# Key pages of the decode, loaded and scored by halves of their buffer during prompt attention

## The reference

```python
k_past = cache_k[page_table, layer].reshape(db, past, N_HEADS_A, HEAD_DIM)
...
s = jnp.einsum('bqhd,bkhd->bhqk', q, k, preferred_element_type=jnp.float32) * ATTN_SCALE
s = s + jnp.swapaxes(c_q, 1, 2)[:, :, :, None] - jnp.swapaxes(c_k, 1, 2)[:, :, None, :]
s = jnp.where(k_pos[None, :] <= q_pos[:, None], s, -jnp.inf)
p = jax.nn.softmax(s, axis=-1)
```

## Time and profile before

| | us |
|---|---|
| three runs | 1713.23, 1716.95, 1719.72 |
| median | 1716.95 |
| the profiled execution | 1712.27 |
| its span (first to last instruction) | 1710.4 |
| TensorE busy with matmuls | 1623.9 (95%) |
| TensorE loading weights | 977.1 |
| DVE, ACT, POOL busy | 805.5, 486.5, 121.1 |
| mean granted clock of TensorE | 0.984 of full |

### The profile page before, as it was taken

How to read it: one execution, slowest core, us unless ns; L and a number is a source line. 1 busy time by engine, 2 the same in 40 slices (tenths; PEclk the granted TensorE clock), 3 DMA queues, 4 the chain that set the end, 5 groups by cost and what they waited for, 6 DMA issues and landing times.

```text
span 1710.4 us, 32596 instructions
## 1 busy us (share of the span) xinstructions
PE 1623.9 (95%) x13510; PEld 977.1 (57%) x13510; DVE 805.5 (47%) x1778; ACT 486.5 (28%) x948; POOL 121.1 (7%) x166
## 2 busy tenths in 40 slices
PE   6999999999999999999989989989999998999998
PEld 3555555555555555568655655568788853444443
DVE  5560299963222244441166665534545556333332
ACT  5301100001024532400155654443233462010001
POOL 1100100011100000100000000000000002122220
PEclk9999999999999999999989999999999999999999
DMA  6233231247631305573075455577575478799983
GB/s 257 90 110 123 100 123 39 75 138 193 189 106 60 124 40 223 215 254 119 16 236 158 127 159 152 152 227 230 163 220 175 152 274 310 282 326 351 349 316 129
DMA packets 150893, 302.87 MB, mean 177 GB/s; under 512 B 16821, under 2 KB 121477, under 8 KB 132374
## 3 DMA queue, kind: packets, MB, share of 16 engines
q1 hardware_dynamic: 128810, 155.65, 29.1%
q0 software_dynamic: 17280, 117.18, 19.2%
q10 hardware_dynamic: 4656, 27.96, 4.0%
HBM read 237.88 MB, written 65.10 MB: 177 GB/s over the span
## 4 chain that ended last, share of the span: by engine, by line
PE 67%; DVE 14%; DMA 6%; SPq 5%; ACT 4%; issue 3%; ACTq 0%; DVEq 0%
PE psum L854 29%; PE psum L1106 21%; DVE big L1871 9%; SPq L578 4%; PE psum L1069 4%; PE psum L935 4%; PE psum L825 3%; PE psum L1030 2%; PE psum L1055 2%; PE psum L880 2%; DMA big<-in_k_pages 1%; ACT big L1530 1%; DMA zst<-in_x_prompt 1%; DMA big<-in_aux 1%; PE psum L1314 1%
## 5 line engine op out<-in xcount | busy, mean ns | idle before, releaser
L854 PE MATMUL psum<-big,wbuf 128*128 128x416 f32 x1920 | 677.4, 514 | 12.2 <-DVE big L1777 11.0
L854 PEld LDWEIGHTS psum<-big,wbuf 128*128 128x128 f32 x1920 | 365.4, 191 | 318.7 <-issue 313.9
L1106 PE MATMUL psum<-big 64*64 64x64 f32 (+3 forms) x5456 | 266.0, 273 | 19.8 <-DVE big L2307 6.5
L1106 PEld LDWEIGHTS psum<-big 64*64 64x64 f32 (+2 forms) x5456 | 183.4, 134 | 108.5 <-issue 75.1
L1503 ACT ACTIVATE zst<-psum 128x416 f32<-128x416 f32 x123 | 63.0, 517 | 533.5 <-PE psum L854 533.4
L1871 DVE SCALAR_TENSOR_TENSOR big<-big,pars 128x2048 f32<-128x2048 f32 x120 | 148.2, 1298 | 1.1
L725 POOL DMA_INDIRECT big<-in_cache_v,pidx x64 | 63.8, 997 | 718.4 <-PE psum L1069 485.6
L825 PE MATMUL psum<-ident,big 128*128 128x128 f32 (+1 forms) x556 | 79.7, 283 | 12.1 <-ACT big L1734 4.0
L1760 ACT ACTIVATE big<-zst 128x1024 f32<-128x1024 f32 (+1 forms) x17 | 17.3, 1020 | 257.4 <-DVE zst L2395 207.7
L2395 DVE TENSOR_TENSOR zst<-zst,psum 128x512 f32<-128x512 f32 x49 | 33.7, 688 | 106.3 <-PE psum L1106 80.0
L825 PEld LDWEIGHTS psum<-ident,big 128*128 128x128 f32 (+1 forms) x556 | 61.8, 146 | 29.4 <-issue 12.7
(11 more groups left out here) (306 smaller groups left out, 1697.3 us busy)
## 6 DMA issues: line engine op xcount, KB each, us to landing
big<-in_k_pages SPq DMA_DIRECT2D x432, 128.0 KB, 2.3
zT<-zst ACTq DMA_DIRECT2D x25, 1040.0 KB, 6.1
wbuf<-in_w_slots SPq DMA_DIRECT2D x24, 512.0 KB, 4.1
big<-zT POOLq DMA_DIRECT2D x11, 1024.0 KB, 5.4
zst<-in_k_pages SPq DMA_DIRECT2D x80, 128.0 KB, 2.7
rwS<-big POOLq DMA_DIRECT2D x8, 1024.0 KB, 4.2
big<-rwS SPq DMA_DIRECT2D x8, 1024.0 KB, 5.7
zst<-in_x_prompt SPq DMA_DIRECT2D x16, 512.0 KB
```

Of the source, the lines that this page charges most:

```text
L854: last = nc.tensor.matmul(psum[:, m % CHUNKS, 0:CW], w[:, k, :], x, start=(k == 0), stop=(k == KT - 1))
L1106: return nc.tensor.matmul(out, l, r, start=start, stop=stop, skip_group_check=True)
```

## The change

Each early key step is cut in two. The first half takes the eight matmuls of the even sequences, the second those of the odd ones.

- SP: the 16 page numbers of a step are read into registers before any wait. Then SP waits until the first eight matmuls of the step in the buffer are done (`k_half`) and issues the eight pages of the even sequences; then it waits for `sc_mm` as before and issues the eight odd ones. The two halves are counted on semaphores of their own. Both are semaphores used earlier in the program (`x_in[4]`, `lf_stored`; `k_half` is `ss_mm`), so before the first early load SP now also waits for an old transfer of `lf_stored`.
- TensorE: the first half stands one block earlier in the item, behind the transposes of the last but one block and what follows them. It carries the waits for `o_read` and for DVE's reading of the step before. The second half stands where the whole step stood, and waits for its own eight pages alone.
- The order of the 16 matmuls, the 16 pages and their sizes, and the other 16 key steps are unchanged.

```diff
+        k_early_in, K_EARLY0 = (x_in[4], lf_stored), (X_SEEN[4], 16 * DEC_BATCH + 16)
+        k_half, K_HALF0 = ss_mm, CHUNKS
...
             def key_pages(k):
-                if k < KEARLY:
-                    if k > 0:
-                        sp.wait_ge(sc_mm, k)
-                elif k - KEARLY >= NRING:
+                if k - KEARLY >= NRING:
                     sp.wait_ge(sc_mm, k - NRING + 1)
...
+                if k < KEARLY:
+                    for half in range(2):
+                        if k > 0:
+                            sp.wait_ge(*((k_half, K_HALF0 + k) if half == 0 else (sc_mm, k)))
+                        for n in range(half, 16, 2):
+                            page_load(k_early, n, k_early_in[half])
...
-            def key_step(k, bank, pages):
-                if k > 0:
+            def key_step(k, bank, pages, half=None):
+                if k > 0 and half != 1:
                     pe.wait_ge(sc_read, k)
-                for n in range(4):
+                for n in range(4) if half is None else (2 * half, 2 * half + 1):
...
-                last.then_inc(sc_mm, 1)
+                if half == 0:
+                    last.then_inc(k_half, 1)
+                else:
+                    last.then_inc(sc_mm, 1)
...
-                pe.wait_ge(k_early_in, K_EARLY0 + 256 * (k + 1))
-                pe.wait_ge(o_read, j)
-                key_step(k, 6 + (j + 1) % 2, k_early)
+                pe.wait_ge(k_early_in[half], K_EARLY0[half] + 128 * (k + 1))
+                if half == 0:
+                    pe.wait_ge(o_read, j)
+                key_step(k, 6 + (j + 1) % 2, k_early, half)
...
-                if j in KEYS_AT:
-                    early_keys(j)
+                    if j in KEYS_AT and c >= blocks(j) - 2:
+                        early_keys(j, c - blocks(j) + 2)
```

More of the change, by code:

```diff
@@ L439, in build @@
         gate_out = [(mixa_stored[0], 0), (mixa_stored[1], 0), (s_in, 16)]
-        k_early_in, K_EARLY0 = x_in[4], X_SEEN[4]
         idx_ready = sem("idx_ready")
         lf_stored = sem("lf_stored")
+        k_early_in, K_EARLY0 = (x_in[4], lf_stored), (X_SEEN[4], 16 * DEC_BATCH + 16)
+        k_half, K_HALF0 = ss_mm, CHUNKS
         k_in = [sem(f"k_in{n}") for n in range(NRING)]
@@ L575, in key_pages, with page_load @@
                     skip_runtime_bounds_check_because="page_table holds page numbers of the cache by its definition")
-                to, s = (k_early, k_early_in) if k < KEARLY else (k_ring[(k - KEARLY) % NRING], k_in[(k - KEARLY) % NRING])
-                for n, page in enumerate(pages):
-                    sp.dma_start(to[:, n % DEC_BATCH, n // DEC_BATCH, :, :], I['k_pages'][bass.ds(page, 1)].rearrange("o p r c -> (o p) r c")).then_inc(s, 16)
+                def page_load(to, n, s):
+                    sp.dma_start(to[:, n % DEC_BATCH, n // DEC_BATCH, :, :], I['k_pages'][bass.ds(pages[n], 1)].rearrange("o p r c -> (o p) r c")).then_inc(s, 16)
+                if k < KEARLY:
[5 more added lines that the diff above has]
+                else:
+                    for n in range(16):
+                        page_load(k_ring[(k - KEARLY) % NRING], n, k_in[(k - KEARLY) % NRING])
             for j in range(len(ITEMS) - 2):
                 if j == 2:
+                    sp.wait_ge(lf_stored, 16 * DEC_BATCH + 16)
                     key_pages(0)
@@ L1070, in key_step, with early_keys @@
                                                 pages[:, b, :, pr, :], start=(n == 0), stop=(n == 3), skip_group_check=True)
-                last.then_inc(sc_mm, 1)
-            def early_keys(j):
+                if half == 0:
+                    last.then_inc(k_half, 1)
+                else:
+                    last.then_inc(sc_mm, 1)
+            def early_keys(j, half):
                 k = KEYS_AT.index(j)
-                if k == 0:
+                if k == 0 and half == 0:
                     pe.wait_ge(qbd_ready, 1)
-                pe.wait_ge(k_early_in, K_EARLY0 + 256 * (k + 1))
-                pe.wait_ge(o_read, j)
-                key_step(k, 6 + (j + 1) % 2, k_early)
+                pe.wait_ge(k_early_in[half], K_EARLY0[half] + 128 * (k + 1))
+                if half == 0:
+                    pe.wait_ge(o_read, j)
+                key_step(k, 6 + (j + 1) % 2, k_early, half)
             scores(0, 0)
```

## The result

| | us |
|---|---|
| change, six runs | 1692.87 to 1701.51, median 1697.37 |
| before, six runs beside it | 1713.23 to 1719.72, median 1716.23 |
| ratio | 0.9891, 95% interval 0.987 to 0.9912 |
| its profiled execution, and its span | 1701.51, 1699.6 |

The change is faster by 18.9 us between the medians; the forecast was 1699.5, 17.5 us under the median of before as it was known then. The two profiled executions differ by only 10.8 us: of the change it is the slowest of the six, and that of before (1712.27) lies under all six of its own.

The account below looks back on a forecast made before the run. A closed 14.5 us loop refilling the single early key buffer stalls TensorE. Terms -13.4 - 3.3 - 2.8 + 1.2 + 0.8 = -17.5 took 1712.27 to 1694.8; 4.7 for the median gave 1699.5, range 1693 to 1709.

Parts of the forecast that it names:

- Loads by halves: Early key steps: refilling even and odd pages separately removes all 13.4 us of TensorE's waits for key pages (bounds 7.1 and 13.4).
- The slack of 2.2 and 1.2 us: Item 22, shortest period: first-half pages back at 7.7 us, wanted at 9.9; second-half pages back at 11.8, wanted at 13.0.
- Page numbers ahead of the wait: SP's register loads: 0.97 us leaves the loop each time, hidden behind TensorE's work, priced at nothing beyond the emptied stalls.
- Clock: Windows of items 24 and 27: the lower clock after stalls no longer comes, -3.3 us (lower bound 1.9).
- Start of RWKV: TensorE's 3.19 us idle for pair 0's loads: 1.6 goes, plus 1.2 for a likely avoided clock fall; -2.8 (0 to 4.8).
- Cost on TensorE: Cut key steps: group changes in items 17 to 30 cost +1.2 us; delayed first halves in items 8 to 15, +0.8.
- Sum: Whole kernel: -13.4 - 3.3 - 2.8 + 1.2 + 0.8 = -17.5 us, for a forecast of 1699.5.
- the rival that named such waits: Softmax loop: delayed last transposes make ACT the bound, every step passing the delay on; +14 us, 1731, chance 0.05.
- the wait did not move to the middle: First halves, mid-item: pages held up by the second half's arrive late, 7 us come back; 1706.5, chance 0.14.
- SP's first issue: SP's queue: over 0.3 us behind the first half's last matmul signals wrong; gate-store rival, only register loads help: 1707.5, chance 0.11.
- Issue was the pace: Page refill: the opposing rival said transfers set the pace, so halves change nothing and cost 2.0 us; 1719, chance 0.04.
- Waiting late: First half's wait, 3.1 us earlier in the item against 2.2 us of slack: by the skill's advice, the wrong place.

## Why the prediction was right, point by point

- **Loads by halves, -13.4.** Right in size: 13.4 us of waits became 0. The slack of 2.2 and 1.2 us was right in kind (with 0.97 more in the loop nothing came back) and too small: it was 3.7 and 2.1 us in the same item. With both halves at the end, where I left up to 0.9 us per long stall, nothing came back either, if only by 0.1 us. I had counted 3.4 us from the last issue to its landing in each step, the largest I had read; over the 16 steps of before it is 2.1 to 3.5, with a median of 2.6.
- **Page numbers ahead of the wait, 0 beside the halves.** Right, by both experiments: 6.2 us of waits left with this alone (6.3 worked out, and in part luck), no change when taken from the halves.
- **Clock, -3.3.** Right for this pair of profiles: no fall is left between 1000 and 1120. No fall is left there in the other two profiles of the change either. In the second profile of before the falls lie behind other stalls (3.24 and 2.73 us), also twice.
- **Start of RWKV, -2.8.** I had 1.6 us of idling left; the three profiles show 1.0, 1.9 and 1.3. The fall of the clock behind it is gone in the first (1.00 in its window) and in the third, but not in the second, where it came behind 1.92 us. The reason I had given for its going, that 1.6 us is far shorter than any stall with a fall behind it, does not hold in the trace of before already, where a fall follows a stall of 1.55 us. That this part of the term came out in the first profile was luck. What I had not thought of is that the load can be put first; that takes the rest.
- **Cost on TensorE, +1.2 and +0.8.** 2.0 and 0.7. The first was mis-sized. A change of group costs 0.14 us in each item from 19 on, and not 0.1 of the idle 0.17 of the earlier trace rows. Item 17 costs 0.5, most of it the wait of item 16 for ACT, which had no term; it is the only sign of the rival that named such waits. The second was right: item 11 costs 0.44 us (0.4 to 0.5 forecast), item 13, built alike, 0.40, and items 8 and 15 nearly nothing.
- **Sum, -17.5.** S went from 280.6 to 263.6, -17.0, and from 280.0 to 263.3 in the second pair; between the medians it is -18.9, with an interval of -15 to -22. For the first pair the measured terms are -13.4 (pages), -3.3 (clock), -2.2 (idle time ahead of RWKV) and +2.7 (cut), -16.2 together; 0.8 us of S, 0.3 of them ahead of the end of the first key step, have no term. The fall of the clock that did not come behind RWKV's start lies outside S.
- **The rivals.** No first half waited for pages, even with the loads whole, so the wait did not move to the middle. SP's first issue followed the first half's last matmul by 0.2 us in the items from 17 on; only in the four short ones did the gate store hold it, for 0.8 to 1.1 us, and there was time. Issue was the pace: it is the term that the halves overlapped. The Trainium skill, "DMA: Bandwidth & Descriptors", section "Issuing engines are not separate DMA queues", holds here for a single page, with 0.51 us from issue to issue against 2.3 us (median) to landing. It says nothing of many in a row, and the prediction went too far in taking it as a rule on the whole refill: issues add up and landings overlap, so 16 issues take 8.1 to 10.2 us and the last page lands 2.1 to 3.5 us after its own. ACT kept almost 3 us of slack, so the softmax loop did not become the bound.
- **Waiting late.** The Trainium skill, the same page, "Rules for kernel authors", advised against the earlier place of the first half. The wait never came due, so the harm was not the one I weighed. But the place cost 2.7 us of TensorE's time and bought only margin (2 us in the shortest items), and over the stage the late place was the better one; over the whole time the two cannot be told apart.

## What to carry to other kernels

When a nearly full engine is off the chain, look for a closed loop: a single buffer whose refill waits for its last reader. Add up its parts (reader, setting up, issues, landing) and compare with the period; each part taken out helps until the loop is shorter than the period, and from then on nothing more is to be had, so parts do not add. Release the buffer piece by piece as it is read, take set-up work out of the wait, and leave the reader where it was: moving half of it cost time here, and releasing half-way through was enough. It was enough by 0.1 us, though: by the same sum, a loop with more in it would need the earlier place as well. No run shows that case. On a queue that issues for several consumers, put first what is wanted first.

## What the runs showed of the hardware that I had not expected

In prompt attention with key steps the clock fell behind stalls of 3.05, 3.06, 3.24 and 3.59 us, but also behind 2.73 and 2.67, and it did not behind 3.03 and 2.64. At the start of RWKV it fell behind 1.92, 2.8, 3.2, 3.3, 3.4 and 3.5 us and did not behind 0.99, 1.3, 1.4, 1.8 and 2.4. The length of a stall alone does not tell. A key step behind a fall took 2.81 to 3.64 us in place of 1.93.

The RWKV stage, the same instructions on TensorE each time, took 224.7 to 234.8 us over all kernels and 226.2 to 234.8 over three profiles of one. A profile of one execution can so differ from the next by nearly 9 us in a stage that no one has touched, half of what this change brings; comparing stages found in one profile what the whole span hid.

In item 22 of the change it took about 0.5 us from one page's issue to the next and 2.0 to 2.7 us from a page's issue to its landing, yet for 16 in a row the issuing queue was the slower part (8.7 us). Reading the 16 page numbers took 0.97 us.
